# State-space outputs of a decoder kernel: lag weights turned through memory, the skip folded into the lag-0 kernel, full-width weights for the chunk sums

## What is computed

```python
u = (h @ w_in).astype(f32)                      # (B, 256, 2048)
ug = u.reshape(B, T, SSM_NGROUPS, SSM_GROUP)    # 128 groups of 16 channels
...                                             # lb: decay, bb = coef * b, 64 complex states a group
bu_re = jnp.einsum('tgc,gpc->tgp', ug, bb_re)
bu_im = jnp.einsum('tgc,gpc->tgp', ug, bb_im)
_, _, xr, xi = lax.associative_scan(_ssm_combine, (ar, ai, bu_re, bu_im), axis=0)
y = einsum('tgp,gcp->tgc', xr, c_re) - einsum('tgp,gcp->tgc', xi, c_im)
y = y.reshape(B, T, D_MODEL) + d_skip.astype(f32) * u
g = jax.nn.gelu(y).astype(h.dtype)
g = g * jax.nn.sigmoid(g @ w_gate)
return g @ w_out
```

## Time and profile before

| | |
|---|---|
| median of three executions | 2725.12 us |
| the profiled execution's own time | 2722.05 us |
| its span in the profile | 2720.3 us |
| busy: PE, weight loads of PE, DVE, ACT, POOL | 2654.6, 2374.8, 2300.6, 1295.7, 514.9 us |
| the stream `ssm_in` with its state-space work | about 1616 to 1790 us of the span |

### The profile page before, as it was taken

How to read it: one execution, slowest core, us unless ns; L and a number is a source line. 1 busy time by engine, 2 the same in 40 slices (tenths; PEclk the granted TensorE clock), 3 DMA queues, 4 the chain that set the end, 5 groups by cost and what they waited for, 6 DMA issues and landing times.

```text
span 2720.3 us, 50038 instructions
## 1 busy us (share of the span) xinstructions
PE 2654.6 (98%) x18416; PEld 2374.8 (87%) x18416; DVE 2300.6 (85%) x3379; ACT 1295.7 (48%) x1869; POOL 514.9 (19%) x468
## 2 busy tenths in 40 slices
PE   6999999999999999999999999999999999999998
PEld 2999888888898888888889999999888888888887
DVE  6978988888889999899999998998898975677754
ACT  2444444444434555435555344444365553455543
POOL 4142211101132111000111321244411110011122
PEclk8999999999999999999999999999999999999999
DMA  9989989888866987678887967879777766655663
GB/s 379 394 262 345 342 316 344 307 315 335 317 226 221 323 283 249 204 248 311 281 285 264 375 229 245 240 252 329 248 263 248 257 184 188 196 189 186 183 188 117
DMA packets 242267, 725.47 MB, mean 267 GB/s; under 512 B 51106, under 2 KB 60066, under 8 KB 241186
## 3 DMA queue, kind: packets, MB, share of 16 engines
q1 hardware_dynamic: 185184, 666.46, 71.3%
q10 hardware_dynamic: 56900, 56.54, 6.5%
HBM read 701.66 MB, written 25.44 MB: 267 GB/s over the span
## 4 chain that ended last, share of the span: by engine, by line
PE 83%; DVE 4%; POOL 1%; issue 1%; ACT 1%; DMA 0%; ACTq 0%; DVEq 0%; POOLq 0%
PE proj L1936 40%; PE proj L1939 22%; PE proj L1959 5%; PE proj L1961 4%; PE proj L1960 4%; PE proj L1941 3%; PE proj L1954 2%; DVE w_lo L1201 1%; PE proj L1957 1%; PE ps L2077 1%; PE ps L2167 1%; ACT w_hi L605 1%; DVE work L1484 0%; POOL work L1784 0%; POOL work L1786 0%
## 5 line engine op out<-in xcount | busy, mean ns | idle before, releaser
L605 ACT ACTIVATE w_hi<-raw 128x1024 fp32r<-128x1024 f32 (+1 forms) x896 | 933.3, 1044 | 986.4 <-PE proj L1939 353.6
L1201 DVE TENSOR_TENSOR w_lo<-raw,w_hi 128x1024 fp32r<-128x1024 f32 (+1 forms) x896 | 1106.3, 1237 | 281.6 <-ACT w_hi L605 269.4
L1936 PE MATMUL proj<-h_hl,w_hi 128*128 128x512 f32 x3990 | 1007.5, 393 | 2.7 <-DVE x L1531 1.8
L1936 PEld LDWEIGHTS proj<-h_hl,w_hi 128*128 128x128 f32 x3990 | 730.5, 189 | 139.2 <-DVE x L1531 2.1
L1939 PEld LDWEIGHTS proj<-h_hl,w_lo 128*128 128x128 f32 x4256 | 580.6, 190 | 41.6
L1939 PE MATMUL proj<-h_hl,w_lo 128*128 128x256 f32 x4256 | 593.4, 282 | 0.0
L1091 DVE SCALAR_TENSOR_TENSOR ada<-ada,held 128x1024 f32<-128x1024 f32 x304 | 392.6, 1291 | 0.0
L1834 POOL TENSOR_TENSOR a_hl<-work,a_hl 128x256 fp32r<-128x256 f32 (+1 forms) x88 | 119.6, 1359 | 1137.9 <-ACT a_hl L895 1137.9
L1959 PE MATMUL proj<-a_hl,w_hi 128*128 128x256 f32 x864 | 245.6, 284 | 0.7 <-DVE a_hl L1422 0.6
L1960 PE MATMUL proj<-a_hl,w_hi 128*128 128x256 f32 x864 | 244.5, 283 | 0.0
L1961 PE MATMUL proj<-a_hl,w_lo 128*128 128x256 f32 x864 | 244.5, 283 | 0.0
(11 more groups left out here) (279 smaller groups left out, 2873.4 us busy)
## 6 DMA issues: line engine op xcount, KB each, us to landing
raw<-in_w_up SPq DMA_DIRECT2D x352, 512.0 KB, 4.9
ada<-in_ada_t SPq DMA_DIRECT2D x304, 512.0 KB, 5.6
raw<-in_w_in SPq DMA_DIRECT2D x224, 512.0 KB, 6.6
raw<-in_w_down SPq DMA_DIRECT2D x128, 448.0 KB, 3.5
raw<-in_w_down SPq DMA_DIRECT2D x64, 512.0 KB, 3.7
ada<-in_ada_w SPq DMA_DIRECT2D x48, 512.0 KB, 8.9
raw<-in_w_out SPq DMA_DIRECT2D x32, 512.0 KB, 5.2
raw<-in_ssm_w_in SPq DMA_DIRECT2D x32, 512.0 KB, 4.8
```

The costliest lines, as they stand in the source:

```text
L605: nc.scalar.activation(w_hi[:, j % LAG, 0:nk * P], raw[:, j % s.ring, 0:nk * P], ACT.Copy).then_inc(hi_ready, 1)
L1201: V.tensor_tensor(w_lo[:, j % LAG, 0:nk * P], raw[:, j % s.ring, 0:nk * P], w_hi[:, j % LAG, 0:nk * P].bitcast(F32), ALU.subtract).then_in ...
L1936: ins = mm(both, w_hi[:, j % LAG, w], hl[:, k].rearrange("p c t -> p (c t)"), start=(k == 0), stop=False)
```

## The change

Only the state-space part changes. In words:

- **Outputs.** `kd`, `spread_k` and the four large products go. The kernel of block n is copied by ACT (`spread_lags`, step 2n+6, one copy of 128x256 out of PSUM through an overlapping window, so that zeros stand where a lag is negative), stored to memory (`store_taps`, 128 KB) and read back (`load_taps`, two DMAs of 64 KB in lines of 256 bytes) as `lagged`, whose rows are channel and place in the chunk, as those of `u_rows`. `outputs` does 16 products of 32 columns of weights and 64 moving ones in their place; `u_rows` has four places instead of two.
- **Skip.** `skip` goes from DVE. In `kernels_of` a third product of 16 columns per quarter adds d_skip on the diagonal (`ident` by `d_own`) at lag 0. `gelu` reads PSUM directly, at 2n+12.
- **Chunk sums.** `bp` is laid out block-diagonally with zeros, so that one product of 128 rows by 128 columns takes the place of two of 64 by 64: 8 products instead of 16. `bp` comes in two DMAs of 64 partitions.
- **Order.** `kernels_of` moves from step 2n+5 of PE to 2n+1. The loads of `bp`, `cp`, `bst` and `tab` from block 2 on move from ACT to SP, at steps 2n+9, 2n+8 and 2n+10. `widen_c` goes from 2n+9 to 2n+8. `magnitudes` goes from POOL to ACT (2n+6). POOL clears the widened tables once.

The diff, cut to its core (the old forms of moved functions and the buffers' places are left out):

```diff
+            def store_taps(n):
+                def f(i):
+                    sp.wait_ge(kw_made, n + 1)
+                    wait(sp, lag_ld[n % 2], 32 * (n // 2))
+                    sp.dma_start(kw_d[n % 2].rearrange("(p j) f -> p (j f)", j=CHUNK),
+                                 lag_rows[:, n % 2].rearrange("p j o k -> p (j o k)")).then_inc(kw_out, 16)
+            def load_taps(n):
+                def f(i):
+                    sp.wait_ge(s5_clear, 2)
+                    wait(sp, y_done, n - 1)
+                    sp.wait_ge(kw_out, 16 * (n + 1))
+                    by_group = kw_d[n % 2].rearrange("(q g m) f -> g m q f", q=4, g=2)
+                    for g in range(2):
+                        sp.dma_start(lagged[g * SP_:(g + 1) * SP_, n % 2, :, g, :], by_group[g]).then_inc(lag_ld[n % 2], 16)
+            def load_cp(n):
+                def f(i):
+                    wait(sp, kb_done, n - 1)
+                    wait(sp, cw_made, n - 1)
+                    sp.dma_start(cp[:, n % 2].rearrange("p a b c -> p (a b c)"), cp_d[n]).then_inc(cp_ld[n % 2], 16)
+                    sp.dma_start(bst[:, n % 2].rearrange("p a b c -> p (a b c)"), a["ssm_bs"][n]).then_inc(cp_ld[n % 2], 16)
...
+            for n in range(KT):
+                late.setdefault(2 * n + 11, []).append(store_taps(n))
+                late.setdefault(2 * n + 12, []).append(load_taps(n))
+                if n > 1:
+                    late.setdefault(2 * n + 9, []).append(load_bp(n))
+                    late.setdefault(2 * n + 8, []).append(load_cp(n))
+                    late.setdefault(2 * n + 10, []).append(load_tab(n))
+            carry = weights("ssm_in", lambda i, b: a["ssm_w_in"][b], late=late, keep=True)
...
+            def spread_lags(n):
+                def f(i):
+                    act.wait_ge(kb_done, n + 1)
+                    act.wait_ge(own_made, 3)
+                    wait(act, kw_out, 16 * (n - 1))
+                    nc.scalar.activation(lag_rows[:, n % 2], k_windows[n % 2], ACT.Copy).then_inc(kw_made, 1)
...
-                late.setdefault(2 * n + 9, []).append(widen_c(n))
-                if n + 2 < KT:
-                    late.setdefault(2 * n + 9, []).append(ahead(load_bp, n + 2))
-                    late.setdefault(2 * n + 10, []).append(ahead(load_cp, n + 2))
-                    late.setdefault(2 * n + 10, []).append(ahead(load_tab, n + 2))
-                late.setdefault(2 * n + 13, []).append(gelu(n))
+                late.setdefault(2 * n + 6, []).append(magnitudes(n))
+                late.setdefault(2 * n + 6, []).append(spread_lags(n))
+                late.setdefault(2 * n + 8, []).append(widen_c(n))
+                late.setdefault(2 * n + 12, []).append(gelu(n))
...
                     for q in range(4):
                         for r in range(2):
-                            for g in range(2):
-                                rows = slice(g * SP_, (g + 1) * SP_)
-                                ins = mm(e_ps[n % 2][rows, r, q, :], bp[rows, n % 2, q, r, :], u_rows[rows, n % 2, q, :],
-                                         start=True, stop=True)
+                            ins = mm(e_ps[n % 2][:, r, q, :], bp[n % 2][:, q, :, :, r].rearrange("p g s -> p (g s)"), u_rows[:, n % 4, q, :],
+                                     start=True, stop=True)
...
+                        ins = mm(k_ps[n % 2][rows, :, CHUNK - 1], ident[:, rows], d_own[:, n, :], start=False, stop=True)
...
-                    for k in range(CHUNK):
-                        mm(y[:, k * NCH:T], kd[:, n % 2, k].rearrange("p g o -> p (g o)"),
-                           u[:, n % 4, 0:CHUNK - k, :].rearrange("p j a -> p (j a)"), start=(k == 0), stop=False)
+                    for j in range(CHUNK):
+                        for q in range(4):
+                            mm(y[32 * q:32 * q + 32, j * NCH:(j + 1) * NCH], lagged[:, n % 2, q].rearrange("p g (o k) -> p (g o) k", k=CHUNK)[:, :, CHUNK - 1 - j],
+                               u_rows[:, n % 4, q, :], start=(j == 0), stop=False)
...
-                late.setdefault(2 * n + (4 if n == KT - 1 else 5), []).append(kernels_of(n))
+                late.setdefault(2 * n + 1, []).append(kernels_of(n))
```

More of the change, by code:

```diff
@@ L516, in _, with weights @@
                     early_piece(e)
-            def weights(name, src, done=0):
+            def weights(name, src, done=0, late=None, carry=None, keep=False):
                 s = st[name]
@@ L545, in load, with load_tab, load_bp, f @@
                             early_piece(e)
-                run_steps(sp, s.count, s.length, load, {}, done=done)
+                return run_steps(sp, s.count, s.length, load, late or {}, done=done, carry=carry, keep=keep)
+            def store_taps(n):
[4 more added lines that the diff above has]
+                                 lag_rows[:, n % 2].rearrange("p j o k -> p (j o k)")).then_inc(kw_out, 16)
+                return f
+            def load_taps(n):
[6 more added lines that the diff above has]
+                        sp.dma_start(lagged[g * SP_:(g + 1) * SP_, n % 2, :, g, :], by_group[g]).then_inc(lag_ld[n % 2], 16)
+                return f
+            def load_tab(n):
+                def f(i):
+                    wait(sp, x_made, n - 1)
+                    sp.dma_start(tab[:, n % 2].rearrange("p a b c -> p (a b c)"), tab_d[n]).then_inc(tab_ld[n % 2], 16)
+                return f
+            def load_cp(n):
[4 more added lines that the diff above has]
+                    sp.dma_start(bst[:, n % 2].rearrange("p a b c -> p (a b c)"), a["ssm_bs"][n]).then_inc(cp_ld[n % 2], 16)
+                return f
+            def load_bp(n):
+                def f(i):
+                    wait(sp, e_done, n - 1)
+                    for g in range(2):
+                        rows = slice(g * SP_, (g + 1) * SP_)
+                        sp.dma_start(bp[n % 2][rows, :, g].rearrange("p q s r -> p q (s r)"),
+                                     bp_d[n][rows].rearrange("p (q f) -> p q f", q=4)).then_inc(bp_ld[n % 2], 16)
+                return f
             def ffn(layer):
@@ L565, in _ @@
             ffn(0)
[L566 to L567 removed]
+            late = {}
+            for n in range(KT):
[6 more added lines that the diff above has]
+            carry = weights("ssm_in", lambda i, b: a["ssm_w_in"][b], late=late, keep=True)
+            weights("gate", lambda i, b: a["ssm_w_gate"][b], carry=moved(carry, {7: 6, 8: 6, 9: 7, 10: 7}))
             weights("ssm_out", lambda i, b: a["ssm_w_out"][b])
@@ L949, in _, with load_first @@
             act.wait_ge(lo_ready, st["ssm_in"].base)
-            load_bp(0)
-            load_cp(0)
-            load_tab(0)
+            def load_first(n):
+                act.wait_ge(s5_clear, 2)
+                for g in range(2):
+                    rows = slice(g * SP_, (g + 1) * SP_)
+                    act.dma_start(bp[n][rows, :, g].rearrange("p q s r -> p q (s r)"),
+                                  bp_d[n][rows].rearrange("p (q f) -> p q f", q=4)).then_inc(bp_ld[n], 16)
+                act.dma_start(cp[:, n].rearrange("p a b c -> p (a b c)"), cp_d[n]).then_inc(cp_ld[n], 16)
+                act.dma_start(bst[:, n].rearrange("p a b c -> p (a b c)"), a["ssm_bs"][n]).then_inc(cp_ld[n], 16)
+                act.dma_start(tab[:, n].rearrange("p a b c -> p (a b c)"), tab_d[n]).then_inc(tab_ld[n], 16)
+            load_first(0)
             norm(2, 1, 0, following="ssm_in")
-            load_bp(1)
-            load_cp(1)
-            load_tab(1)
+            load_first(1)
             s = s5 = st["ssm_in"]
```

200 lines of the change are left out of this document (97 added, 103 removed).

## The result

The change makes the kernel slower: 2829.9 us median (2824.72 to 2834.34, six executions) against 2725.6 (2721.68 to 2727.33, six), ratio 1.039, 95% interval 1.038 to 1.040. The forecast was 2761.5 with a range to 2787: the sign and the wait that decides were right, and the size was off by a factor of 2.6 (+39.5 expected, +102.6 between the two spans, 2822.9 against 2720.3). A part of the size is a mechanism that the forecast had left to a rival: PE's clock falls behind each wait.

The account below looks back on a forecast made before the run. PE bounded the kernel before; late loads would make PE wait in every block. Start 10.6, twelve periods 28.3, last wait 2.6, then -2.8, +1.5 and -0.7 gave +39.5 on 2722.05: 2761.5 us, range 2740 to 2787.

Parts of the forecast that it names:

- the loads' new place: `kernels_of` at PE's piece 2n+1 leaves one piece between the loads' issue and use, where three lay: PE waits 2.5 us.
- the wait's name: On PE's chain ahead of L2229: DMA from `in_ssm_bs` or `cp_d`, some 2.5 us, fourteen times, the first of ten.
- the price of the 16 chunk sums: PE's chunk sums per block: 16 instructions at 0.11 make 1.76 us, against 1.07 before, covered by the wait.
- `bst` is issued at 4.09: SP's issue of `bst` in each block, 4.09 us after PE's end of an even piece.
- I keep 4.2: Time from `bst`'s issue to its landing in each block: 4.2 us, with bounds of 3.0 and 5.5.
- K: Time from PE's end of an even piece to `bst` landed: 8.3 us, bounds 7.1 and 9.6.
- Kernels 0.37 + 0.11: PE's `kernels_of` in each block: 0.37 us as before, plus 0.11 for four more products.
- Rival 3, the clock: PE's clock falls again in every block of the stream: +23 to +28 us, 2785 to 2790; chance 0.08.
- 8.3 + 0.48 + 3.23 = 12.0: The new block: `bst` landed, then kernels, then time to PE's next release; 12.0 us against 9.64.
- shift at the release of piece 6: Delay at the stream's start: 7.6 for the loads, 0.5 for chunk sums, 2.5 for the low clock; 10.6 us.
- twelve periods: Blocks from the release of piece 6 to that of piece 30: 12 x (12.0 - 9.64) = 28.3 us.
- rest to the end: Stream's end: last wait 2.6, four outputs -2.8, three chunk sums +1.5, skip -0.7 us.

Follow-up runs that it names:

- e5b: The kernel before with only the loads of `bp`, `cp`, `bst` and `tab` issued by SP at the change's steps: 2725.6 us, ratio 1.000.
- e11: The change with `load_cp` (`cp` and `bst`) issued first where SP's loads fall on one step: 2803.4 us, ratio 1.030 to the kernel before.
- e4: The change with 18 unused identity products added ahead of PE's wait in each block from the third on: 2811.9 us, ratio 1.032 to the kernel before.
- e8b: e7b with contiguous chunk-sum weights and `load_cp` first on SP: 2724.9 us, ratio 1.000 to the kernel before.
- e2: e1 with the chunk sums again as 32 instructions with 64x64 weights: 2735.3 us, ratio 1.004 to the kernel before.
- e7b: e2 with the lag kernels in PSUM by lag and channel, so operand and output are contiguous: 2738.8 us, ratio 1.005 to the kernel before.
- e9: e8b with `bp` read in one load and block 1's read of `u` issued earlier: 2722.1 us, ratio 1.000 to the kernel before.
- e6b: The change with the chunk sums again as 32 instructions of 64x64 weights: 2827.2 us, ratio 1.037 to the kernel before.
- e10: The change with the lag kernels in PSUM by lag and channel, so contiguous: 2826.8 us, ratio 1.039 to the kernel before.
- e1: The change with `kernels_of` two pieces later, at 2n+3, and `spread_lags` one step later: 2740.5 us, ratio 1.006 to the kernel before.

## Why the prediction was right and wrong

Right: what decides (the loads' new place), the wait's name, its fourteen times, its place in the program, the bound moving from PE to SP's chain, the weights' issue at 2.34, the price of the 16 chunk sums (1.76 forecast, 1.79 measured) and that it is hidden. Wrong: three terms of the block's sum were mis-sized, and the clock was left out of it.

- **"`bst` is issued at 4.09".** It is 5.19 or 5.20 in every block that the chain shows: +1.10. Here the two tap reads and `tab` hold SP for about 0.6 each. The reading of the earlier trace rows failed: they show 0.33 for `cp` and for the weight piece, each the first issue after a pause, and no row of `tab`. The same timeline of the kernel before has the issues behind `cp`:

```profile
1683.17 0.46 ACTq L938 DMA_DIRECT2D ada<-in_ssm_bs  x1
1683.72 0.51 ACTq L931 DMA_DIRECT2D raw<-tab_d  x1
```

So part of this error could be read before the run: `tab` took 0.51 in this very block, and 0.33 to 1.26 in the stream. It is not only its shape: the same transfer takes 0.60 behind the tap reads in the change, and 0.43 behind a weight piece in most blocks of e5b.
- **"I keep 4.2" for the landing.** Eleven landings on the chain, 1684.98 to 1845.83, average 4.96: +0.76. The landings lie between 3.8 and 6.3, and I took one row for all. With both terms K is 10.16, outside my bounds of 7.1 to 9.6. e11 tests the issue: 1.53 off it took 1.46 off K, and 26.5 us off the time. Why the landing is longer stays open. That `bst` closes the burst is not the cause by itself, since in e11 it does not and takes 5.04.
- **"Kernels 0.37 + 0.11".** 1.25 at full clock. From the kernels' start to the next release is 4.50 (1756.64 to 1761.14 in e4), not 3.71: +0.79. I counted instructions and left out that `cp` is now read across its rows, and PSUM written so; contiguous forms give 0.46 of it back (0.79 in e8b), and the other 0.31 against my 0.48 was not taken apart. The Trainium skill, "PSUM — Partial Sum Buffer", table of specifications, says that non-contiguous patterns slow products significantly. The runs agree at full clock (1.25 against 0.79); they don't part the output's stride from the operand's.
- **Rival 3, the clock, with 0.08.** It came on top of the forecast instead of in its place. From the earlier trace rows I read that an idle of 2.45 left the clock at 1.00. That was so, over the 5 us behind it too, but one idle was no ground for a chance of 0.08: the change has the low clock already behind the 2.1 us for DVE at its start (products 0.21 apart from 1630.50 on), and e11 behind three of seven waits as short. In the change all fourteen waits, 2.8 us and more, have it. The kernels' start plus 4.50 would end the block at 10.16 + 0.04 + 4.50 = 14.70; it ends at 16.07, so the low clock costs 1.37 a block. I had priced the rival at 1.7. That it came near is luck: at half the clock 6 us lose 3 us of work, not half of 3.5 (and 13 x 1.7 is 22, not 23). Measured, the clock is low for less than that behind most waits (0.50 to 0.71 over the first 5 us), and the kernels hardly slow down in it (1.37 against 1.25). The wait was already 3.8 with K at 9.6, my own upper bound, and the range to 2787 held no clock on top of that. The Trainium skill, "TensorE: Matmul & The Clock Gate", section on HAM oscillation, describes just this: a wait for data in every tile, and each tile begun at half rate. The trace agrees: the clock is down behind each of the fourteen waits. I had used another section of that page and not this one.

So 8.3 + 0.48 + 3.23 = 12.0 became 10.16 + 0.04 + 4.50 + 1.37 = 16.07. The measured terms are averages, the 16.07 over the eleven blocks from 1679.78 to 1856.56. Over the stream, by the starts of the chunk sums:

| | forecast | measured |
|---|---|---|
| shift at the release of piece 6 | 10.6 | 1661.38 - 1643.52 = 17.9 |
| twelve periods | 28.3 | 194.9 - 116.1 = 78.8 |
| rest to the end | 0.6 | 5.9 |
| sum | 39.5 | 102.6 |

The start failed in the same way. On its chain of waits:

```profile
1641.24 4.87 DMA kw_d<-work
1646.18 0.69 SPq L572
...
1648.23 3.27 DMA ada<-in_ssm_bs
1651.55 0.66 PE pmisc L2229 x6
```

The order is the forecast one: store, two reads, `bst`, kernels. But the store begins at 1641.24 and not at 1637.4, since PE waited 2.1 us for DVE ahead of `kernels_of(0)` and the clock fell behind that wait too, and it took 4.87, not 3.8. The issues took 1.0 more and the landing 0.9 less than forecast, so `bst` was there at 1651.5 and not at 1646.5. The chunk sums begin at 1652.99 and run at the low clock:

```profile
1652.00:1661.00 9.00, 9.00 (x60) 8.96 (x57) 4.23 (x7) 0.00 (x0) 0.00 (x0) 0.50 0.01 2
```

I put 2.5 in for the clock once; nine microseconds of work at 0.50 are 4.5.

On the estimate from the Trainium skill, "DMA: Bandwidth & Descriptors", anatomy of one DMA (K = 7.5): the trace disagrees, 10.16. In the stretch before the landing the DMA engines are at 0.94 and move 299 GB/s, less than the 436 of the fit. The Trainium skill gives that fit for DMAs issued by GpSimd; these are SP's. The Trainium skill, "TensorE: Matmul & The Clock Gate", LDWEIGHTS, gave an estimate of 1.71 for the chunk sums; the trace agrees, 1.79. By the same working the 32 halves of e2, with 64 columns each, would take 1.71 too, and they take 1.11.

What stays open: why `bst` takes 5 us to land, when a short wait is followed by the low clock and when not, and what the `issue` stalls in the chunk sums of e7b to e9 are (1.4 to 4.8 us in a stream), which with the waits for `u` eat the 0.2 a block of e8b and e9. No version was measurably faster than the kernel before.

## What to carry to other kernels

When a load and its use move closer together, compute the landing from the queue's own rows: everything issued ahead of it in that step, each at the price it has behind another issue and not alone, and a range of landings, not one row. Put the load that is awaited first in its step (26 us here), or put the use two pieces later (89 us here), before touching the arithmetic: e6b and e10 saved PE work next to a wait and came out 3 us below the change, with intervals that overlap its own. And where the working puts an idle of 2 us or more into every period, add the price of the low clock to the forecast itself, not to a rival beside it.

## What was not expected of the hardware

- A program that does more work in the place of a wait can be faster: 18 products a block took 18 us off (e4).
- Products whose moving operand and output are not contiguous cost more at full clock and almost nothing at the low one: 24 instructions in 1.25 against 0.79 at 1.00 (e1, e8b), 1.44 against 1.37 at 0.50 behind the wait (the change, e10).
- An idle of 2.07 us was followed by the low clock (e11, at 1796.76) and one of 2.45 was not (the kernel before, at 1639.38).
- The issue of the same load takes longer behind some others: `tab` 0.60 behind the tap reads (the change, e11), mostly 0.43 behind a weight piece (e5b), and 0.33 to 1.26 on ACT before; the two halves of `bp` hold SP for some 1.2 in most blocks and for 2.48 once (at 1862.70 in the change). What sets it was not tried.
